# Differential scores on 64 rows each, GpSimd scaling in the sparse attention, and buffers at multiples of 512 bytes

## What is computed

```python
p_sel = masked_softmax(jnp.einsum('bkgqd,bkqmd->bkgqm', qc, ks) * scale, ...)
o_sel = jnp.einsum('bkgqm,bkqmd->bkgqd', p_sel, vs)
p_win = masked_softmax(jnp.einsum('bkgqd,bknd->bkgqn', qc, kw) * scale, win_mask)
o_win = jnp.einsum('bkgqn,bknd->bkgqd', p_win, vw)
o = gates[0] * o_cmp + gates[1] * o_sel + gates[2] * o_win
```

```python
def probs(qb, k):
    sc = jnp.einsum('bhqd,bhkd->bhqk', qb, k).astype(jnp.float32) * scale
    sc = jnp.where(mask, sc, -jnp.inf)
    return jax.nn.softmax(sc, axis=-1)
w = probs(qb1, k1) - lam * probs(qb2, k2)
return jnp.einsum('bhqk,bhkd->bhqd', w.astype(v.dtype), v)
```

## Time and profile before

| | |
|---|---|
| median of 3 runs | 3013.3 us (3012.6 to 3014.54) |
| the profiled execution | 3012.69 us, span 3010.6 us |
| granted TensorE clock, mean over the span | 0.983 of full speed |
| VectorE busy | 48% |
| ScalarE busy | 27% |
| weights moved | 446 DMAs of 512 KB, 3.4 us each from issue to landing |

### The profile page before, as it was taken

The page is one execution under the profiler, slowest core; times in us unless marked ns, Lnnn a source line. Parts: engine busy times, 40 slices in busy tenths (PEclk is TensorE's granted clock), DMA queues, the critical chain, the costliest instruction groups (busy, mean ns, idle before and its releaser), DMA issues.

```text
span 3010.6 us, 38240 instructions
## 1 busy us (share of the span) xinstructions
PE 2894.1 (96%) x13750; PEld 2332.4 (77%) x13750; DVE 1454.8 (48%) x2115; ACT 806.1 (27%) x1493; POOL 1976.5 (66%) x2234
## 2 busy tenths in 40 slices
PE   8999999998879999999799999999999999999998
PEld 6887888876757788887677777888877777888887
DVE  3745666046488666631854555222045445533302
ACT  2232222023258522210323432111022344111100
POOL 5747999776710288976844567777676445877764
PEclk8999999998989999999999999999999999999999
DMA  3112222222200122222211122222222111222222
GB/s 137 64 50 84 98 94 94 98 84 74 88 22 2 36 98 94 95 98 87 82 56 60 66 72 95 94 97 98 92 89 71 63 63 64 91 98 97 93 96 91
DMA packets 66359, 242.52 MB, mean 81 GB/s; under 512 B 7488, under 2 KB 7616, under 8 KB 66240
## 3 DMA queue, kind: packets, MB, share of 16 engines
q1 hardware_dynamic: 66240, 240.95, 23.8%
HBM read 238.82 MB, written 2.10 MB: 80 GB/s over the span
## 4 chain that ended last, share of the span: by engine, by line
PE 84%; DVE 12%; ACT 2%; issue 2%; DMA 0%; DVEq 0%; SPq 0%; ACTq 0%
PE bank L444 24%; PE bank L446 23%; PE bank L445 23%; ACT n_t L1200 1%; PE bank L938 1%; PE bank L971 1%; PE bank L848 1%; PE bank L1009 1%; PE bank L822 1%; PE bank L832 1%; DVE XL L1497 1%; DVE ss L1506 1%; PE bank L561 1%; PE bank L723 1%; PE bank L983 1%
## 5 line engine op out<-in xcount | busy, mean ns | idle before, releaser
L432 POOL TENSOR_TENSOR w_lo<-w_raw,w_hi 128x256 fp32r<-128x256 f32 x1784 | 1490.3, 866 | 35.7
L429 POOL CAST w_hi<-w_raw 128x1024 fp32r<-128x1024 f32 x446 | 487.8, 1094 | 970.5 <-DMA w_raw<-weights_dram 969.6
L444 PE MATMUL bank<-XH,w_hi 128*128 128x512 f32 x2416 | 964.5, 399 | 21.4 <-DVE XL L1497 12.6
L445 PE MATMUL bank<-XL,w_hi 128*128 128x512 f32 x2416 | 947.2, 392 | 0.0
L446 PE MATMUL bank<-XH,w_lo 128*128 128x512 f32 x2416 | 947.1, 392 | 0.0
L444 PEld LDWEIGHTS bank<-XH,w_hi 128*128 128x128 f32 x2416 | 457.7, 189 | 125.9 <-DVE XL L1497 19.6
L446 PEld LDWEIGHTS bank<-XH,w_lo 128*128 128x128 f32 x2416 | 457.2, 189 | 97.5
L445 PEld LDWEIGHTS bank<-XL,w_hi 128*128 128x128 f32 x2416 | 457.9, 190 | 94.9 <-issue 3.5
L1511 DVE TENSOR_TENSOR X<-X,bank 128x512 f32<-128x512 f32 x64 | 43.8, 685 | 524.9 <-PE bank L446 524.5
L445 PE MATMUL bank<-hid_l,w_hi 128*128 (+1 forms) x704 | 278.5, 396 | 0.0
L444 PE MATMUL bank<-hid_h,w_hi 128*128 (+1 forms) x704 | 278.5, 396 | 0.0
(11 more groups left out here) (327 smaller groups left out, 3600.7 us busy)
## 6 DMA issues: line engine op xcount, KB each, us to landing
w_raw<-weights_dram SPq DMA_DIRECT2D x446, 512.0 KB, 3.4
x_tok<-x_dram SPq DMA_DIRECT2D x4, 512.0 KB, 5.3
out_dram<-y_tok SPq DMA_DIRECT2D x4, 512.0 KB, 2.7
const_sb<-consts_dram SPq DMA_DIRECT2D x1, 834.0 KB, 11.7
par_sb<-params_dram SPq DMA_DIRECT2D x1, 665.0 KB, 10.2
masks_in<-masks_dram SPq DMA_DIRECT2D x1, 640.0 KB, 12.8
y_gain<-gain_out_dram SPq DMA_DIRECT2D x1, 512.0 KB, 4.5
const_sb<-consts_dram SPq DMA_DIRECT2D x1, 129.0 KB, 2.2
```

Source lines behind the costliest of these rows:

```text
L429: nc.gpsimd.tensor_copy(w_hi[s][:, :, :], w_raw[s][:, :, :]).then_inc(s_hi, 1)
L432: ins = nc.gpsimd.tensor_tensor(w_lo[s][:, rows, :], w_raw[s][:, rows, :], w_hi[s][:, rows, :].bitcast(F32), ALU.subtract)
L444: nc.tensor.matmul(out_ap, w_hi[slot][:, j, :], xh, start=start, stop=False)
L445: nc.tensor.matmul(out_ap, w_hi[slot][:, j, :], xl, start=False, stop=False)
```

## The change

Three things are changed together.

*Differential scores on 64 rows.* `h_dk` loses its axis of two copies and its zeros: the rotation adds all 128 rows at once, and the two memsets go. The scores of half c read rows 64c to 64c + 63 of queries and keys, so each matmul uses half of the array's rows. The stream is cut in two parts of half the width (not at a width of 128), issued as part 1 of half 0, part 1 of half 1, part 2 of half 0, part 2 of half 1; the two masks stand behind all of them.

*Sparse attention.* From job 16 on the scaling runs on GpSimd (`weigh`), which takes it up in its stream of weight splits after the unit `START["nsa_o"] + 3`, in order of the jobs, waiting for the reciprocal (`rc`). VectorE still makes the reciprocals, and copies the transposes of every odd job from PSUM (`tcd`) in place of ScalarE; TensorE waits for the one or the other copy through `copied`.

*Places.* The first byte is rounded up to a multiple of 512 (16896), and `o_A` to a multiple of 128 words, so that `X`, `XH`, `XL`, the ring, and the area A with its buffers begin at multiples of 512 bytes.

```diff
-SBUF_WORDS = 53200
+SBUF_WORDS = 53104
+POOL_WEIGHS = 16
...
-        first_byte = -(-nc.sbuf_base // 32) * 32
+        first_byte = -(-nc.sbuf_base // 512) * 512
...
+        top[0] = -(-top[0] // P) * P
         o_A = words(0)
...
-        h_dk = at("h_dk", [P, 4, 2, T], F32, o_A + 2048)
+        h_dk = at("h_dk", [P, 4, T], F32, o_A + 2048)
...
+            def weigh(m):
+
+                e, i, par, c = m // 16, query_tile(m), m // 2 % 2, m % 2
+                pool.wait_ge(ns["rc"], m + 1)
+                w = n_P[m % 6][:, 0:(i + 1) * P]
+                col = 16 * (c + 1) + 2 * e + par
+                nc.gpsimd.tensor_scalar(w, w, n_st[:, 1, m:m + 1], n_gate[:, i, col:col + 1], ALU.mult, ALU.mult)\
+                    .then_inc(ns["w"], 1)
+
             for u in range(UNITS):
                 split(u % RING, 16 * (u // RING + 1), u + 1)
+                if u == START["nsa_o"] + RING - 1:
+                    for m in range(POOL_WEIGHS, NSA_HEADS * TT * 2):
+                        weigh(m)
...
+                def copied(m):
+                    on_dve = m // 2 - POOL_WEIGHS // 2 + m % 2
+                    if m % 2 and m >= POOL_WEIGHS:
+                        pe.wait_ge(ns["tcd"], on_dve)
+                    else:
+                        pe.wait_ge(ns["tc"], m + 1 - max(0, (m - POOL_WEIGHS + 1) // 2))
...
                         if m >= 3:
-                            pe.wait_ge(ns["tc"], m - 2)
+                            copied(m - 3)
...
-                        pe.wait_ge(ns["tc"], 4 * n + 4)
+                        copied(4 * n + 2)
+                        copied(4 * n + 3)
...
+                    first = S // 2 if i else 0
+                    for lo_, hi_ in ((0, first), (first, S)):
+                        for c in range(2 if lo_ < hi_ else 0):
+                            r = slice(DH * c, DH * (c + 1))
+                            nc.tensor.matmul(bank[4 + c][:, lo_:hi_], h_dq[r, h, i * P:S], h_dk[r, h, lo_:hi_],
+                                             start=lo_ == 0 or first == 0, stop=False, skip_group_check=True)
                     for c in range(2):
-                        b = bank[4 + c]
-                        nc.tensor.matmul(b[:, 0:S], h_dq[:, h, i * P:S], h_dk[:, h, c, 0:S], start=True, stop=False)
-                        nc.tensor.matmul(b[:, i * P:S], ident_bf[:, :], causal_bf, start=False, stop=True)\
-                            .then_inc(hs["s"], 1)
+                        nc.tensor.matmul(bank[4 + c][:, i * P:S], ident_bf[:, :], causal_bf, start=False, stop=True,
+                                         skip_group_check=True).then_inc(hs["s"], 1)
...
-                    if 5 <= q < jobs + 5:
+                    if 5 <= q < jobs + 5 and (q - 5 < POOL_WEIGHS or q % 2):
...
+                    if POOL_WEIGHS + 5 <= q < jobs + 5 and q % 2 == 0:
+                        m = q - 5
+                        n, i = m // 4, query_tile(m)
+                        if m % 4 == 1:
+                            dve.wait_ge(ns["pv"], n - 1)
+                        dve.wait_ge(ns["t"], m + 1)
+                        V.tensor_copy(n_PT[:, n % 2, m % 4, 0:i + 1, :],
+                                      bank[1 + m % 3][:, 0:(i + 1) * P].rearrange("p (j t) -> p j t", t=P)).then_inc(ns["tcd"], 1)
...
-                        own(V.reciprocal(n_st[:, 1, m:m + 1], n_st[:, 1, m:m + 1]))
-                        V.tensor_scalar(w, w, n_st[:, 1, m:m + 1], n_gate[:, i, col:col + 1], ALU.mult, ALU.mult)\
-                            .then_inc(ns["w"], 1)
+                        V.reciprocal(n_st[:, 1, m:m + 1], n_st[:, 1, m:m + 1]).then_inc(ns["rc"], 1)
+                        if m < POOL_WEIGHS:
+                            dve.wait_ge(ns["rc"], m + 1)
+                            V.tensor_scalar(w, w, n_st[:, 1, m:m + 1], n_gate[:, i, col:col + 1], ALU.mult, ALU.mult)\
+                                .then_inc(ns["w"], 1)
...
-                    halves = (slice(0, DH), slice(DH, P))
-                    dst = [(h_dq[:, t, :], slice(0, P))] if t < 4 else [(h_dk[r, t - 4, c, :], r) for c, r in enumerate(halves)]
+                    dst = [(h_dq[:, t, :] if t < 4 else h_dk[:, t - 4, :], slice(0, P))]
...
-                    if t in (1, 2, 9, 10):
+                    if t in (9, 10):
...
-                        V.memset(h_dk[other, :, c, :] if t < 4 else h_sk[other, c:SB_HEADS:2, :], 0.0)
+                        V.memset(h_sk[other, c:SB_HEADS:2, :], 0.0)
```

More of the change, by code:

```diff
@@ L363, in build @@
             "xh2", "xl2", "kh", "kl", "evac", "yh", "yl", "rot", "rope", "vT", "vc", "hid", "hT", "hTc", "kvc", "kvcc", "gT",
-            "gate", "p0", "cs", "csub", "cmax", "ce", "p", "s", "mx", "exp", "w", "t", "tc", "pT", "pTc", "pv", "oh", "o")}
+            "gate", "p0", "cs", "csub", "cmax", "ce", "p", "s", "mx", "exp", "w", "t", "tc", "pT", "pTc", "pv", "oh", "o", "rc", "tcd")}
         hs = {n: sem("hyb_" + n) for n in (
```

## The result

| | before | after |
|---|---|---|
| median | 3013.9 us (4 runs) | 2973.6 us (4 runs, 2972.5 to 2977.7) |
| ratio | | 0.987 (95% interval 0.9858 to 0.9883) |
| span of the profiled execution | 3010.6 us | 2971.1 us |
| granted clock, mean | 0.983 | 0.984 |

The account below looks back on a forecast made before the run. TensorE, busy 96% of the span, was taken as the bound, mostly by the split weight products. 3012.7 - 5 (scores) - 5.3 (rotation) - 7 (sparse attention) - 19.2 (places) = 2976 us, range 2850 to 3002 us.

Parts of the forecast that it names:

- the case that the forecast had as the likeliest: Whole kernel: 2976 us, area matmuls reach 226.7 ns, those on XH and XL unchanged; chance 0.40.
- Part 3, places: Weight products: 2880 matmuls on the area gain 6.7 ns each, -19 us; no change taken for XH and XL.
- (a): Weight products: offset 0 frees XH too, surcharge perhaps growing with distance; 2836 us in full, to about 2906; chance 0.33.
- (d): Weight products: offset 0 is a worse place, XH's matmuls take 6.7 ns more, 3046 us; chance 0.06.
- Rival (b): Weight products: place does nothing, hid slow for its height or nature; 2995 us; chance 0.21 with or without (c).
- Part 1, the scores: Differential scores on TensorE: halves overlap, 0.61 us less a head, -5 us in all; bounds -9 to +11.
- the second pass of one half beside the first of the other: Score passes on row halves: 5 steps for 8 passes, 1.07 us at 512 columns.
- a limit by weight loads: Narrow score units: loads 0.11 us apart, 0.88 us at 384 and 256 columns, 0.44 at 128.
- Rival (c): Differential scores: halves don't run together, 2992 us; chance 0.21 shared with (b), which counts with or without it.
- Part 1, the rotation: Waits for h_raw: -3.3 us in layer 0, -2.0 in layer 1, together -5.3 us (-3 to -7).
- Half of each goes at least: Three VectorE key-addition pairs in layer 0, 2.56, 2.23 and 1.79 us: 3.3 us goes, TensorE's 10.6 us wait becomes about 7.
- Part 2: Sparse attention: 1.0 to 1.3 us removable for each of 7 head pairs, -7 us; GpSimd scaling about 0.5 us; bounds -9 to +3.

Follow-up runs that it names:

- everything at 32: Changed kernel with the first byte of everything 32 bytes up, so X, XH, XL, ring and area A stand 32 past a multiple of 512: 2974.9 us.
- the area at 384: Kernel before with area A alone moved up 32 bytes, from 352 to 384 past a multiple of 512: 2994.5 us, ratio 0.9935.
- two of the experiments: Changed kernel with GpSimd scaling and all copies on ScalarE: 2973.2 us; changed kernel with GpSimd scaling from job 0, copies shared from job 16: 2972.4 us.

## Why the prediction was right

The forecast was 2976 us and the result is 2973.6; it came by the case that the forecast had as the likeliest. The sum held partly because its errors were of both signs: 36.5 us foretold, 40.3 found.

*Part 3, places: -19.2 us foretold, -19.4 measured alone.* The pace came out as forecast, 226.7 ns on the area and no change on XH. What carried it was the cautious half of the argument, that the area would "come at least to stand as XH stands to the weights now". The reading beside it, distance from a multiple of 512, was wrong: rivals (a) and (d) rested on it, and the kernel with everything at 32 refutes both as mechanisms. Rival (b), that hid is slow for what it is, is refuted by the kernel before with the area at 384. The page SBUF — State Buffer of the Trainium skill, section Operand start alignment, which the prediction named, says that its runs timed nothing, so it has no price for a place. Here a place relative to another costs up to 56 us.

*Part 1, the scores: -5 foretold, -9.2 measured.* The failed step is the shape of the overlap. The prediction took "the second pass of one half beside the first of the other", 5 steps of 8 passes, and for narrow units a limit by weight loads of 0.11 us. In its place: both halves run wholly side by side and 0.21 us is paid on top. At 512 columns both pictures give 1.07 us, which is why that width could not have told them apart; at 128 the prediction's load limit gave 0.44 us, near the measured 0.42, but at 256 it gave 0.88 against 0.65. The masks took 0.12 us (0.11 foretold). The visit to the halves cost 0.30 us, 0.20 by the second passes and 0.10 ahead of the masks, where the sum had 0.17 for the entry alone. Rival (c) didn't come.

*Part 1, the rotation: -5.3 foretold, some -8.2 measured* (waits for h_raw over the span 13.6 with part 1 undone, 5.4 with it). The mis-sized term is "Half of each goes at least": one addition takes 0.69 us where half of the pairs would be 0.9 to 1.3, so 4.5 us went from three of them in place of 3.3. That much is luck of the timing against GpSimd's subtractions: the same three took 1.41 us each in two of the experiments. The wait in the first layer is 5.0 us and not 7, but its 5.6 us less are not all gain. From VectorE's second scaling of the layer (1462.28 us before, 1446.66 after) to the end of the wait it is 43.7 and 39.7 us, 4.0 less; TensorE, counted from the same scaling, comes to the wait 1.6 us later. One cost stood in no sum: the granted clock behind a wait. In the windows view it is the first number behind POOL's; in the kernel before:

```profile
1500.00:1505.00 5.00, 0.00 (x0) 0.00 (x0) 3.73 (x4) 1.18 (x2) 3.79 (x5) 0.50 0.00 0
1505.00:1510.00 5.00, 4.03 (x13) 3.40 (x14) 2.97 (x6) 3.11 (x5) 0.00 (x0) 0.57 0.00 0
```

and in the changed kernel:

```profile
1485.00:1490.00 5.00, 3.63 (x11) 3.05 (x12) 3.02 (x4) 3.11 (x5) 4.65 (x5) 0.53 0.00 0
1490.00:1495.00 5.00, 5.00 (x19) 3.98 (x18) 3.59 (x6) 0.00 (x0) 0.00 (x0) 0.78 0.00 2
```

After the 10.6 us of standing still TensorE works for 3 us at 0.50 of full speed, the lower of its two levels (1.2 GHz), and after the 5.0 us for nearly 6 us: in the first layer the change did not remove this loss. In the second it did. The kernel before has such a stretch behind the wait of 2.0 us:

```profile
2284.00:2286.00 2.00, 2.00 (x7) 1.71 (x8) 0.22 (x1) 1.95 (x4) 1.48 (x3) 0.54 0.41 166
```

It lost some 1.6 us there, by its products at 0.43 us from start to start in place of 0.23. The changed kernel waits 0.3 us at that place and has a granted clock of 1.00. The measured gain of the rotation contains this.

*Part 2: -7 foretold, -4.8 measured.* The failed term is "the removable time at 1.0 to 1.3 us for each of 7 head pairs", which I took above what the waits row has (9.0 - 3.9 = 5.1 us). The row itself was the right size. GpSimd's scaling cost 624 ns on average and not 0.5 us (medians of 447, 553, 660 and 767 ns at 128 to 512 columns, the last as the 769 ns named in the prediction), which hid all the same. And I credited two edits where one pays.

## What to carry to other kernels

Where TensorE is the bound, measure the start-to-start pace of every kind of matmul, not its busy time: equal shapes at different paces pointed here to where their operands lie, and placing streamed operand and weights alike took 672 bytes of each partition. A wait names the engine that finished last, not the one that is short of time: before giving that engine less to do, look at the busiest engine ahead of it in the chain. An edit made of two halves is worth running as halves; here one carried the gain and the other alone cost 5.9 us.

## What was not expected of the hardware

- A matmul of 512 columns in the reduced form takes 226.7 ns from start to start where weights and streamed operand stand alike or 256 bytes apart modulo 512, and 233.3 where they stand 32, 64 or 224 bytes apart; moving the weights by 32 bytes against XH, XL and the area made this kernel 56 us slower.
- Float32 passes on the two row halves of the array overlap whole whatever the order of issue (1.07, 1.06 and 1.07 us at 512 columns), and a visit to the halves costs 0.30 us: 0.20 by the second passes, 0.10 behind the last.
- VectorE's addition of two SBUF operands of 512 columns took 0.68 to 0.69 us beside no subtraction of GpSimd and 1.09 to 1.44 beside one, whether on 64 rows or on 128; the two additions that took 2.56 us were both disturbed.
